# Parameters and x's first quarter loaded first, the first high part on VectorE, the bias table's product in two fp32r parts, and the tail's first mean on GpSimd

## What is computed

```python
for l in range(2):
    x = x + 0.5 * swiglu(rmsnorm(x, g_ff1[l]), w1_ff1[l], w3_ff1[l], w2_ff1[l])   # d_ff 2816
    p = rmsnorm(x, g_mix[l]) @ w_in[l]
    ...
    o_a = diff_attention(..., t5_a, ...)        # 4 heads, T5 relative bias
    o_b = neighborhood_attention(..., na_rpb[l])# 8 heads
    o_c = dilated_attention(..., t5_c)          # 8 heads, T5 relative bias
    x = x + (sum of sigmoid(g_i) * (o_i @ w_br_i[l])) @ w_o[l]
    x = x + 0.5 * swiglu(rmsnorm(x, g_ff2[l]), w1_ff2[l], w3_ff2[l], w2_ff2[l])
return rmsnorm(x, g_final)
```

## Time and profile before

| | us |
|---|---|
| median of 3 runs | 1279.93 |
| lowest and highest of them | 1279.76, 1280.77 |
| the profiled execution, its whole time | 1279.97 |
| its span in the profile | 1278.1 |
| TensorE busy | 1268.8 (99%) |
| VectorE busy | 865.9 (68%) |
| ScalarE busy | 684.4 (54%) |
| GpSimd busy | 43.1 (3%) |

### The profile page before, as it was taken

One profiled execution on the slowest core, in us unless ns is written; L12 is line 12 of the kernel. 1 busy time (PEld: TensorE's weight loads), 2 busy tenths in 40 slices (PEclk: granted clock), 3 DMA queues, 4 the chain that ended last, 5 costly groups with the idle time before them and its releaser, 6 DMA issues.

```text
span 1278.1 us, 17726 instructions
## 1 busy us (share of the span) xinstructions
PE 1268.8 (99%) x6823; PEld 1081.9 (85%) x6823; DVE 865.9 (68%) x1244; ACT 684.4 (54%) x934; POOL 43.1 (3%) x57
## 2 busy tenths in 40 slices
PE   9999999999999999999999999999999999999997
PEld 6888888888888888888888888888888888888886
DVE  6666667656888776566675566765588887655665
ACT  6544455446766455554554544554477653644444
POOL 0411100000000000000000000000000000000000
PEclk9999999999999999999999999999999999999999
DMA  8787755574644545555445555465555454555550
GB/s 294 246 254 248 251 213 191 194 230 153 226 125 176 178 167 196 197 184 181 180 178 197 197 197 185 149 225 186 181 206 194 124 185 178 181 197 197 197 193 38
DMA packets 59213, 245.08 MB, mean 192 GB/s; under 512 B 21344, under 2 KB 27616, under 8 KB 32408
## 3 DMA queue, kind: packets, MB, share of 16 engines
q1 hardware_dynamic: 58144, 242.54, 54.5%
q10 hardware_dynamic: 984, 1.80, 0.5%
q0 software_dynamic: 32, 0.02, 0.0%
HBM read 239.07 MB, written 5.27 MB: 191 GB/s over the span
## 4 chain that ended last, share of the span: by engine, by line
PE 98%; DVE 0%; DMA 0%; issue 0%; ACT 0%; POOLq 0%; POOL 0%; SPq 0%; DVEq 0%; ACTq 0%
PE bank L738 30%; PE bank L705 17%; PE bank L706 16%; PE bank L707 16%; PE bank L742 16%; PE bank L1041 1%; PE bank L796 1%; PE bank L803 1%; PE bank L1055 1%; DMA params<-in_params 0%; DVE x L1492 0%; PE bank L891 0%; PE bank L1078 0%; PE bank L883 0%; DVE xT L1289 0%
## 5 line engine op out<-in xcount | busy, mean ns | idle before, releaser
L1153 DVE TENSOR_TENSOR wlo<-raw,whi 128x2048 fp32r<-128x2048 f32 x209 | 480.0, 2298 | 274.3 <-ACT whi L449 268.5
L449 ACT ACTIVATE whi<-raw 128x2048 fp32r<-128x2048 f32 x206 | 393.6, 1913 | 229.5 <-PE bank L742 143.3
L738 PE MATMUL bank<-xT,whi 128*128 128x512 f32 x1664 | 414.8, 391 | 0.0
L738 PEld LDWEIGHTS bank<-xT,whi 128*128 128x128 f32 x1664 | 301.8, 188 | 55.7 <-issue 0.9
L742 PEld LDWEIGHTS bank<-xT,wlo 128*128 128x128 f32 x1664 | 220.2, 190 | 12.8
L742 PE MATMUL bank<-xT,wlo 128*128 128x256 f32 x1664 | 224.1, 282 | 0.0
L705 PE MATMUL bank<-whi,xT 128*128 128x512 f32 x432 | 171.7, 398 | 0.0
L707 PE MATMUL bank<-whi,xT 128*128 128x512 f32 x432 | 168.6, 390 | 0.0
L706 PE MATMUL bank<-wlo,xT 128*128 128x512 f32 x432 | 168.3, 389 | 0.0
L705 PE MATMUL bank<-whi,hTh 128*128 128x512 f32 x320 | 124.6, 390 | 0.0
L706 PE MATMUL bank<-wlo,hTh 128*128 128x512 f32 x320 | 124.5, 389 | 0.0
(11 more groups left out here) (163 smaller groups left out, 1140.2 us busy)
## 6 DMA issues: line engine op xcount, KB each, us to landing
raw<-in_stream SPq DMA_DIRECT2D x209, 1024.0 KB, 4.8
bias<-t_rows SPq DMA_DIRECT2D x24, 256.0 KB, 6.5
bias<-in_rpb SPq DMA_DIRECT2D x16, 256.0 KB, 7.8
masked<-bias SPq DMA_DIRECT2D x8, 512.0 KB, 7.0
bias<-masked SPq DMA_DIRECT2D x8, 512.0 KB, 4.5
raw<-in_stream SPq DMA_DIRECT2D x10, 256.0 KB, 6.5
x<-in_x SPq DMA_DIRECT2D x4, 256.0 KB, 5.3
raw<-in_stream ACTq DMA_DIRECT2D x2, 256.0 KB, 4.2
```

The costliest lines, as they stand in the source:

```text
L449: act.activation(whi[:, s, :], raw[:, s, :], ACT.Copy).then_inc(hi_ready, 1)
L738: return pe.matmul(dst[blk][:, :], whi[:, s, w], xT[:, 4 * a + k, :, :].rearrange("p a s -> p (a s)"), start=start, stop=stop)
L1153: dve.tensor_tensor(wlo[:, s, :], raw[:, s, :], whi[:, s, :].bitcast(F32), ALU.subtract).then_inc(unit_split, 1)
```

## The change

Five edits. (1) SP's queue begins with the parameters; x's quarter 0 is issued first on ScalarE's queue, ahead of pieces 0 and 1. (2) The high part of piece 0 of unit 0 is made by VectorE with a copy (`first_hi`), not by ScalarE; the counts of `piece_hi` are one lower. (3) The product of the one-hot matrix with the T5 table is made in two fp32r products, of the table's high and low part; ScalarE rounds the one-hot matrix into `onehot_hi` (in `pTh`) and the table into `t5_hi` behind x's squares, for which it waits for `const_landed`; VectorE makes `t5_lo` behind the mean square. (4) TensorE waits for these parts, not for `const_landed`. (5) In the tail, the first two sums and EPS are added by GpSimd in two instructions, and VectorE's instruction for it is gone.

```diff
@@ setup
+        t5_hi = sb("t5_hi", [32, T5_HEADS], F32R)
+        t5_lo = sb("t5_lo", [32, T5_HEADS], F32R)
+        onehot_hi = pTh[0:32, 0, :, :].rearrange("p a b -> p (a b)")
@@ SP
-            load_x(0, 0)
             sp.dma_start(params[:, :, 0:NEGLAM], params_in).then_inc(params_landed, 16)
             load_x(1, 0)
@@ GpSimd, at the end
+            pool.wait_ge(tail_square, 2)
+            pool.tensor_tensor(tail_means[:, 0:1], tail_sums[:, 0:1], tail_sums[:, 1:2], ALU.add).then_inc(early_mean, 1)
+            pool.wait_ge(early_mean, 1)
+            pool.tensor_scalar(tail_means[:, 0:1], tail_means[:, 0:1], EPS, None, ALU.add).then_inc(early_mean, 1)
             for t in range(TILES):
-                pool.wait_ge(tail_mean, t + 1)
+                if t == 0:
+                    pool.wait_ge(early_mean, 2)
+                else:
+                    pool.wait_ge(tail_mean, 1)
                 pool.tensor_tensor(tail_scale[:, t:t + 1], tail_means[:, t:t + 1], minus_half[:, 0:1], ALU.pow).then_inc(tail_rstd, 1)
@@ ScalarE
+            act.dma_start(x[:, 0, 0:512], x_in[0, 0:P, 0:512]).then_inc(x_landed[0], 16)
             for k in range(2):
                 w = slice(k * 512, (k + 1) * 512)
                 act.dma_start(raw[:, slot_of(0), w], stream[0, :, w]).then_inc(piece_landed[k], 16)
...
                     load_constants()
                     squares(l, inst)
+                    act.wait_ge(const_landed, 48)
+                    act.activation(onehot_hi, v[0:32, 0, 0, :], ACT.Copy).then_inc(t5_high, 1)
+                    act.activation(t5_hi[:, :], t5_sb[:, :], ACT.Copy).then_inc(t5_high, 1)
...
-            piece_to_hi(0, 0)
             act.wait_ge(params_landed, 16)
             first_quarter(0)
             piece_to_hi(0, 1)
@@ TensorE
+                    if u == k == 0:
+                        pe.wait_ge(first_hi, 1)
+                    elif k < 3:
+                        pe.wait_ge(piece_hi, 3 * u + k)
...
-                    pe.wait_ge(const_landed, 48)
-                    pe.matmul(bank[1][0:T5_HEADS, :], t5_sb[:, :], v[0:32, 0, 0, :], start=True, stop=True).then_inc(t5_product, 1)
+                    pe.wait_ge(t5_high, 2)
+                    pe.wait_ge(t5_split, 1)
+                    pe.matmul(bank[1][0:T5_HEADS, :], t5_hi[:, :], onehot_hi, start=True, stop=False)
+                    pe.matmul(bank[1][0:T5_HEADS, :], t5_lo[:, :], onehot_hi, start=False, stop=True).then_inc(t5_product, 1)
@@ VectorE
                     mean_squares(l, j)
+                    dve.wait_ge(t5_high, 2)
+                    dve.tensor_tensor(t5_lo[:, :], t5_sb[:, :], t5_hi[:, :].bitcast(F32), ALU.subtract).then_inc(t5_split, 1)
...
+            dve.wait_ge(piece_landed[0], 16)
+            dve.tensor_copy(whi[:, slot_of(0), 0:512], raw[:, slot_of(0), 0:512]).then_inc(first_hi, 1)
             piece_to_lo(0, 0)
...
             tail_residual(3, 1, 0, 512, 1)
-            dve.wait_ge(tail_square, 2)
-            dve.scalar_tensor_tensor(out=tail_means[:, 0:1], in0=tail_sums[:, 0:1], scalar=EPS, in1=tail_sums[:, 1:2], op0=ALU.add,
-                                     op1=ALU.add).then_inc(tail_mean, 1)
             tail_residual(4, 1, 512, 512, 3)
```

More of the change, by code:

```diff
@@ L167, in build @@
         masked = nc.dram_tensor("masked", [DEPTH * BLK, P, 2 * TILES * S], F32, kind="Internal").ap()
+        t5_high, t5_split, first_hi, early_mean = map(sem, ("t5_high", "t5_split", "first_hi", "early_mean"))
         raw_landed = [sem(f"raw_landed{s}") for s in range(SLOTS)]
@@ L807, in block_ready @@
                     pe.wait_ge(late if k == 3 else early, n_quarter(0, 0, q) if k == 3 else 3 * q + k + 1)
-                def piece_ready(u, k, early, late, credit):
-                    pe.wait_ge(late if k == 3 else early, n_unit(0, u) + credit if k == 3 else 3 * u + k + 1)
                 def both_hi(u, k, t):
                     block_ready(block_hi, quarter_hi, u, k, t)
-                    piece_ready(u, k, piece_hi, hi_ready, 0)
+                    if u == k == 0:
+                        pe.wait_ge(first_hi, 1)
+                    elif k < 3:
+                        pe.wait_ge(piece_hi, 3 * u + k)
+                    else:
+                        pe.wait_ge(hi_ready, n_unit(0, u))
                     product(u, k, t, xTh, whi, start=u == k == 0)
                 def weights_lo(u, k, t, stop=False):
-                    piece_ready(u, k, piece_split, unit_split, CREDIT)
+                    if k < 3:
+                        pe.wait_ge(piece_split, 3 * u + k + 1)
+                    else:
+                        pe.wait_ge(unit_split, n_unit(0, u) + CREDIT)
                     return product(u, k, t, xTh, wlo, stop=stop)
@@ L1140, in piece_to_lo @@
                 if k < 3:
-                    dve.wait_ge(piece_hi, 3 * u + k + 1)
+                    if u == k == 0:
+                        dve.wait_ge(first_hi, 1)
+                    else:
+                        dve.wait_ge(piece_hi, 3 * u + k)
                 else:
```

## The result

| | before | after |
|---|---|---|
| median, us (20 runs each) | 1280.65 | 1282.85 |
| lowest and highest | 1279.69, 1282.02 | 1279.85, 1284.15 |
| ratio after / before | | 1.0015 [1.0009, 1.0021] |
| the profiled execution, whole time | 1279.97 | 1279.94 |
| its span | 1278.1 | 1278.2 |

The kernel became 2.2 us slower at the medians. That is less than the 0.2% set as the bound, so "no change" holds as a class, but the interval of the ratio leaves 1 out, and the time lies outside the predicted range of 1278.8 to 1280.6. The two profiled executions are equal, and this is the first thing to read here: the one of after is among the shortest of its twenty. Eighteen of the twenty took 1281.51 to 1284.15 us. The profile can therefore show the loss only in part.

What follows compares the result with a forecast made beforehand. TensorE was taken as the bound, 98% of the chain that ended last. Opening 0, bias table -0.3 after the new wait and tail -0.08 gave -0.4 us, from 1279.97 to 1279.6; range 1278.8 to 1280.6.

Steps and rivals of the forecast that it cites:

- the tail: End of the kernel: without VectorE's mean the fourth residual and everything behind it come 0.08 us earlier (bounds 0, -0.16).
- Opening: 0: First 10 us: the new loads and VectorE's copy leave the product at 9.12 unmoved (bounds -0.3 and +0.8).
- The wait for the biased row: Before the first down projection: TensorE waits for VectorE's row, so only about 0.3 of the 0.50 us is kept.
- just in time at 29.4: VectorE before the biased row: its other work ends about 29.4, just as ScalarE's high part of unit 5 ends (29.31).
- The opening ends later: Opening: the first weight piece lands late and delays quarter 1's transposes; up to +0.4 us, 1280.4; chance 0.17.
- ScalarE becomes the bound: Around the bias table: late tables or costlier copies delay ScalarE; with tables at 21.5, +0.5 us, 1280.5; chance 0.10.
- the covers: Around the bias table: ScalarE's lateness is covered by 1 us (gated values), 0.35 (unit 3's low part), 2 (tables).
- The shorter product only waits: Before the first down projection: biased row 0.3 us later, no gain but the tail's, 1279.9; chance 0.08.
- More is kept: Opening to first down projection: first weight piece lands at 5.1, unit 5's load earlier, more gain kept; 1279.0; chance 0.10.

Runs made afterwards that it cites:

- e1: The change measured again, unedited, on another chip: 1281.13 us, ratio to before 1.0003 [0.9994, 1.0011].
- e13: The change again, unedited, as a single execution: 1281.63 us.
- e14: The change again, unedited, as another single execution: 1281.85 us.
- e9: The change measured again, unedited, in another series: 1282.89 us, ratio to before 1.0015 [1.0006, 1.0024].
- e5: The change with x's second quarter issued ahead of the parameters on SP: 1281.80 us, ratio to before 1.0008 [0.9999, 1.0017].
- e11: The change with weight piece 1 issued on SP behind x's second quarter: 1281.79 us, ratio to before 1.0006 [0.9996, 1.0015].
- e3: The kernel before with only the new order of loads and VectorE's copy: 1282.16 us, ratio to before 1.0015 [1.0006, 1.0023].
- e8: The kernel before with only the new order of loads: 1282.00 us, ratio to before 1.0008 [0.9999, 1.0017].
- e16: The change with VectorE's bias row moved ahead of its low part of unit 5: 1281.38 us, ratio to before 1.0005 [0.9996, 1.0014].
- e4: The change with the old order of loads: 1280.31 us, ratio to before 0.9995 [0.9986, 1.0003].
- e2: The change with the old order of loads and the first high part back on ScalarE: 1280.49 us, ratio to before 0.9995 [0.9987, 1.0004].

## Why the prediction was wrong

**What held.** The parameters land first (4.2), the first weight piece at 5.4 as said, VectorE's copy took 0.427 where 0.487 was worked out: 0.83 ns per element with its fixed part. `t5_lo` took 0.16, GpSimd's two operations 0.19 and 0.23, the tail gave 0.06 for 0.08, and between the first down projection and the tail nothing moved. Of the 3.2 us between 1279.6 and 1282.85, 0.7 is the base: the prediction counted from 1279.97, and the kernel before has a median of 1280.65 over twenty runs.

**The step that failed is the opening, "Opening: 0".** The 32 products came 0.73 us late in the profile, and 1.25 to 1.40 late in e1, e13 and e14. Two landings were not worked out. For x's second quarter the prediction carried over the 4.8 us of the earlier trace rows and let it land earlier because it was issued 0.4 earlier. It took 5.9, and 5.6 to 6.1 in eight of the nine other traces with the change's order of loads; e9 alone had 4.9. With the old order it took 4.3 to 5.3 in six traces. For weight piece 1 it had no term at all: it asked only what becomes of the piece that moves from first to second place, and not of the one that moves from second to third. That piece took 5.8 to 6.9 us (4.9 in e9), and was issued 0.4 us later, against 4.1 to 4.4 with the old order. In e5 and e11 another order only moved the lateness on to another transfer. The Trainium skill (DMA: Bandwidth & Descriptors, "Issuing engines are not separate DMA queues") says that transfers share the same 16 DMA engines and interleave, whichever engine issued them, and these traces agree with it; the prediction had weighed it and named as the payer the first piece, which landed at the 5.4 it was given.

Why the DMA engines are slower is not settled. From 1.5 to 7 us they moved 1.33 MB in the profile after and 1.50 MB before; the parameters' small packets now go first there, but no run shows that these are the cause.

**A term was missing, TensorE's clock.** No rival had it, since the granted clock of the kernel before is 1.00 throughout its opening. With an idle stretch near 8 us it falls to 0.50 in e3, e8 and e16 for three to four us, and costs 1.3 (3.88 against 2.54). It is not certain in any one run: e11 was idle from 8 to 9 (busy 0.00) and kept its clock, and so did e5, idle from 5.5 to 7.6. The wide pitch until about 10 us costs 0.7 in e13 and makes the opening of e4 late too, at a granted clock that reads 1.00. The Trainium skill (TensorE: Matmul & The Clock Gate, "What's actually happening") has the lower clock as the default state that activity lifts, with a transition that varies between runs of one kernel. The pitches here agree: every trace starts at 0.43 us, and the traces of the change leave it between 5.0 us (e9) and 10 us (e1, e13, e14). Added to e16's opening of 14.96, what follows the opening in e13 (1279.8 - 13.40 = 1266.4) gives a span of 1281.4, 1283.2 us whole: the usual time of the change in its two slower series. This is put together from two executions; none of the change itself near 1283 was caught in a trace, so how the loss of 2.2 us divides between landings, pitch and the fallen clock stays open.

**The wait for the biased row** was the right mechanism with the wrong size. The prediction let it take 0.2 of 0.5 us; the product gave 0.40, and the wait took 0.24 in the profile, close to that, but 0.95 + 0.24 in e13, 1.19 + 0.24 in e14, 0.63 + 0.24 in e1 and 1.39 + 0.24 in e2. It is not of the change alone: e8, with the product unsplit, has 1.77 of it. The size hangs on unit 4's load, 5.1 us in the profiled execution of before and 8.4 in e13. The prediction's "just in time at 29.4" was read from one execution, one in which that load was early. In seven of the eleven traces with part 3 and the row in its old place the wait took more than the 0.40 that the product gave. The product's gain is lost there, but the rest of the wait is not part 3's doing, as e8 shows; over many runs e2 and e4, which have part 3 and the old loads, lie 0.6 and 0.8 us below before at the medians.

**The rivals.** "The opening ends later" is what happened, with other payers and a larger price: +0.7 to +2.8 us at the 32 products in all traces with the new loads but e9's, not +0.4 at the end; part of it is the pitch, which makes e4 late by 1.2 with the old loads. "ScalarE becomes the bound" is seen once, in e9: tables landed at 21.64, which the rival had priced at 21.5, with waits for the gated values and unit 3's low part. In the other traces the covers held. "The shorter product only waits" is true as well, in the mildest of cases. "More is kept" was seen in none.

## What to carry to other kernels

When a transfer is put at the head of a queue, write down the new landing of every transfer behind it and who waits for each, for here the one that moved from second to third place paid some 1.5 us in every trace of the change but e9's. A gain taken from a chain is only kept if the next feeder has slack in other executions than the profiled one; look for the longest landing that feeder can meet, and reorder the feeder's queue (here one addition ahead of one low part) together with the change. Short stalls of TensorE in an opening can cost more than themselves, through its clock, in some runs and not in others, and a single profile will not show it. Look at the distance of its products beside the granted clock, for here the two did not always agree.

## What the hardware showed that was not expected

- Filler products whose output nobody reads made the kernel faster by 1.7 us (1282.89 to 1281.18, same chip). No run with them had a mean granted clock under 0.998; four of the eleven without them had 0.996.
- Products of 512 columns start 0.43 us apart at first in every trace, at a granted clock that reads 1.00, and step to 0.23 between 4.4 us (e11) and some 10.5 us (e5).
- The same kernel had medians of 1282.85, 1281.13 and 1282.89 in three series, with x's second quarter and weight piece 1 landing in 4.9 to 6.0 us.
- One 1 MB load took 4.9 to 5.2 us when it was issued ahead of two small loads of another queue and up to 9.6 us when it was issued behind them. Both orders occur among the executions of the change.
- The end of the span comes 3.08 us after the start of ScalarE's last store issue in the kernel after, and 3.06 to 3.08 in the thirteen other executions with the mean on GpSimd, but 3.42 to 3.45 in the four whose tail is that of before. The stores land alike (2.7 us), and the traces have the difference between the last two semaphore events of GpSimd, 0.43 us apart in the kernel before and 0.09 after. These 0.35 us, more than the 0.08 predicted for the tail, belong to the tail's edit by that division; why is not shown.
